# Two transformer blocks on one core: the gates' chains interleaved, signals per block, entry rows on ScalarE, the store in parts

## The reference, cut to what matters

```
for layer in range(2):
    hl = modulate(rmsnorm(xl, norm_g[layer, 0]), mod_l[0], mod_l[1])   # and hc from xc
    yc, yl = even_mixer(...) if layer % 2 == 0 else rwkv_mixer(...)
    xl = xl + mod_l[2] * rmsnorm(yl, norm_g[layer, 1])
    hl = modulate(rmsnorm(xl, norm_g[layer, 2]), mod_l[3], mod_l[4])
    xl = xl + mod_l[5] * rmsnorm(conv_ffn(hl, ...), norm_g[layer, 3])
    ...   # the same for xc and hc, where not last
rwkv_project: xx = shifted - h;  xr, xw, xk, xv, xa, xg = (h + xx * mu[i] for i in range(6))
```

## Time and profile before

| | |
|---|---|
| median of 3 runs | 3086.62 us (3085.43 to 3086.74) |
| profiled execution: its own time, its span | 3089.13 us, 3087.3 us |
| busy: TensorE, VectorE, ScalarE | 2873.1 us (93%), 1645.6 us (53%), 1219.4 us (39%) |
| mean granted clock of TensorE | 0.957 of full |
| bytes moved by DMA | 349.82 MB, 113 GB/s on average |

### The profile page before, as it was taken

One profiled execution on the slowest core, in us unless ns is written; L12 is line 12 of the kernel. 1 busy time (PEld: TensorE's weight loads), 2 busy tenths in 40 slices (PEclk: granted clock), 3 DMA queues, 4 the chain that ended last, 5 costly groups with the idle time before them and its releaser, 6 DMA issues.

```text
span 3087.3 us, 64784 instructions
## 1 busy us (share of the span) xinstructions
PE 2873.1 (93%) x27888; PEld 2405.2 (78%) x27888; DVE 1645.6 (53%) x2475; ACT 1219.4 (39%) x1856; POOL 112.9 (4%) x152
## 2 busy tenths in 40 slices
PE   8999999999999997998877999997998999998997
PEld 8977799899777996776656777784456998985986
DVE  5546555455465544312564777646233554565885
ACT  5445554444455444323443432333203434432333
POOL 0000000000000000000000000000001222220000
PEclk9999999999999998997988999998999999999999
DMA  6544345455443543541001243321210000002442
GB/s 247 184 170 167 123 164 182 166 184 184 170 161 117 178 175 115 188 151 69 2 10 55 106 154 138 121 86 48 96 44 26 5 4 24 5 4 110 148 146 103
DMA packets 49981, 349.82 MB, mean 113 GB/s; under 512 B 5793, under 2 KB 5793, under 8 KB 9249
## 3 DMA queue, kind: packets, MB, share of 16 engines
q1 hardware_dynamic: 49248, 343.56, 31.3%
q0 software_dynamic: 448, 2.11, 0.2%
HBM read 344.61 MB, written 1.05 MB: 112 GB/s over the span
## 4 chain that ended last, share of the span: by engine, by line
PE 80%; DVE 13%; ACT 4%; issue 2%; DMA 1%; DVEq 0%; ACTq 0%; SPq 0%
PE psum L165 79%; DVE arena L98 3%; DVE ring_low L87 2%; DVE arena L87 2%; DVE wide L87 1%; ACT w_high L144 1%; ACT arena L140 1%; DMA ring<-in_evt 1%; PE psum L170 1%; DVE wide L98 1%; ACT x_high L138 1%; DVE ring L87 0%; ACT L138 0%; DVE h L98 0%; ACT arena L144 0%
## 5 line engine op out<-in xcount | busy, mean ns | idle before, releaser
L87 DVE TENSOR_TENSOR ring_low<-ring,w_high 128x2048 fp32r<-128x2048 f32 (+3 forms) x254 | 560.3, 2206 | 565.3 <-ACT w_high L144 560.8
L144 ACT ACTIVATE w_high<-ring 128x2048 fp32r<-128x2048 f32 (+3 forms) x254 | 468.9, 1846 | 794.9 <-PE psum L165 482.6
L165 PE MATMUL psum<-x_high,w_high 128*128 128x256 f32 (+1 forms) x2040 | 634.5, 311 | 11.9 <-DVE x_low L87 6.5
L165 PE MATMUL psum<-x_high,ring_low 128*128 128x256 f32 (+1 forms) x2040 | 627.5, 308 | 0.0
L165 PE MATMUL psum<-x_low,w_high 128*128 128x256 f32 (+1 forms) x2040 | 627.3, 308 | 0.0
L165 PEld LDWEIGHTS psum<-x_high,w_high 128*128 128x128 f32 x2040 | 390.9, 192 | 50.1 <-issue 17.1
L165 PEld LDWEIGHTS psum<-x_high,ring_low 128*128 128x128 f32 x2040 | 390.8, 192 | 18.6
L165 PEld LDWEIGHTS psum<-x_low,w_high 128*128 128x128 f32 x2040 | 390.9, 192 | 16.9
L165 PE MATMUL psum<-wide,ring 64*64 64x64 f32 (+3 forms) x3888 | 385.2, 272 | 19.2 <-DVE wide L98 9.7
L165 PEld LDWEIGHTS psum<-wide,ring 64*64 64x64 f32 (+2 forms) x3888 | 270.7, 147 | 115.4 <-issue 90.8
L165 PE MATMUL psum<-w_high,x_high 128*128 128x512 f32 (+2 forms) x720 | 281.3, 391 | 9.9 <-issue 8.0
(11 more groups left out here) (196 smaller groups left out, 3444.1 us busy)
## 6 DMA issues: line engine op xcount, KB each, us to landing
ring<-in_f_gu SPq DMA_DIRECT2D x88, 1024.0 KB, 4.8
ring<-in_w_mod SPq DMA_DIRECT2D x48, 1024.0 KB, 5.0
ring<-in_fu SPq DMA_DIRECT2D x44, 1024.0 KB, 4.9
ring<-in_f_dn SPq DMA_DIRECT2D x40, 1024.0 KB, 4.8
ring<-in_w_in SPq DMA_DIRECT2D x28, 1024.0 KB, 4.8
ring<-in_fd SPq DMA_DIRECT2D x20, 1024.0 KB, 4.9
ring<-in_rkvr SPq DMA_DIRECT2D x12, 1024.0 KB, 4.8
ring<-in_w_out SPq DMA_DIRECT2D x8, 1024.0 KB, 4.8
```

What stands on the lines that cost most here:

```text
L87: self.done(self.eng.tensor_tensor(o, a, b, op), then)
L144: self.done(self.eng.activation(o, i, ACT.Copy, scale=scale), then)
L165: ins = self.eng.matmul(o, l, r, start=a, stop=z)
```

## The change

Five things:

- Gates that come in pairs (before FFN 4 and before the recurrent mixer): the context gate's squares, factors and products of half n=1 are done between the copies of the latent gate's blocks. `gates_end` then orders VectorE: additions of the context gate, factors of the latent one between them, one product, the first norm's factors, the other product, the additions of the latent gate, the second norm's factors. ScalarE's root of the latent gate lies between the squares of the first norm.
- The signals of squares (`gs_ok`) and additions (`ga_ok`) are given per token block. The small Sqrt stands before the squares of half n=0, for all gates but the latent one of evo.
- The single gates (recurrent mixer, FFN 5): token block 0 of half 1 is multiplied ahead of the factors. The clearing of the image tiles for FFN 5 moves from its start to the end of the recurrent mixer.
- RAW norms: all eight rows k are written by ScalarE; `norm_rows` goes. VectorE's differences wait for pairs of rows or single rows, and the mixes are made between them. The norm before FFN 5 joins `SHARED`. The RAW norms' scratch moves to another buffer.
- The store of `h` goes out in four DMAs of 256 KB, each behind its addition.

```diff
 CONV = (("c", 4, 1), ("c", 4, 0))
-SHARED = (("e", 1), ("e", 0)) + CONV
+SHARED = (("e", 1), ("e", 0)) + CONV + (("c", 5, 0),)
...
 xt_mm = signal("xt_mm", [(q, k) for q in NORMS for k in range(8)])
-xh_ok = signal("xh_ok", [(q, k) for q in NORMS for k in range(0, 8, 2 if q in RAW else 1)])
+xh_ok = signal("xh_ok", [(q, k) for q in NORMS for k in range(8)])
 xw_ok = signal("xw_ok", [(q, k) for q in SHARED for k in (0, 2, 4, 6)])
-xr_ok = signal("xr_ok", [(q, k) for q in RAW for k in (1, 3, 5, 7)])
...
+    if q == ("c", 5, 0):
+        return x_whole[:, k, :]
...
         se.wait_ge(*md_ok[1 if q[0] == "r" or q[1] == 5 else 0, 1 if q[0] == "c" else 0])
-    for k in range(0, 8, 2 if q in RAW else 1):
+    for k in range(8):
...
     if i == 4:
-        A.act(nsmall(CONV[0])[:, 20:21], ident[:, 0:1], ACT.Sqrt)
-        for q in CONV:
-            norm_squares(A, q, 0)
-            norm_squares(A, q, 1)
-            norm_root(A, q)
+        norm_squares(A, CONV[0], 0)
+        gate_root(A, GATES[1])
+        norm_squares(A, CONV[0], 1)
+        norm_root(A, CONV[0])
+        for n in range(2):
+            norm_squares(A, CONV[1], n)
+        norm_root(A, CONV[1])
...
                 A.copy(CY[:, tb, 512 * n:512 * n + 512], bank(down_bank(i, n, tb)), ya_ok((i, n, tb)))
-    for q in GATED[i]:
-        gate_squares(A, q, 1)
-    for q in GATED[i]:
-        gate_root(A, q)
+                if n and tb == 0:
+                    gate_squares(A, GATED[i][0], 1)
+    if i >= 4:
+        gate_root(A, GATED[i][0])
+    if i == 4:
+        gate_squares(A, GATED[i][1], 1)
...
     norms = norms_of(i)
-    if i == 5:
-        D.fill(IMG, 0.0)
-        D.fill(IMC, 0.0, cleared(i))
...
             D.copy(CY[:, tb, 512 * n:512 * n + 512], bank(down_bank(i, n, tb)), yd_ok((i, n, tb)))
-    if i != 4:
-        gates_dve(D, GATED[i])
+            if i == 4 and n and tb == 1:
+                gate_factors(D, GATES[2])
+                gate_mult(D, GATES[2], 1)
+            if i == 5 and n:
+                gate_mult(D, GATES[5], 1, (0,))
+                gate_end(D, GATES[5])
...
     dst, y, col, w, scr, sm, b = gate_of(q)
-    if n:
+    if n == 0 and (q[0], q[-1]) != ("e", 0):
...
         A.eng.wait_ge(*gate_ready(q, n, j))
-        A.act(scr, y[:, j, 512 * n:512 * n + 512], ACT.Square, gs_ok((q, n)) if j else None, scale=1.0 / 32,
+        A.act(scr, y[:, j, 512 * n:512 * n + 512], ACT.Square, gs_ok((q, n, j)), scale=1.0 / 32,
...
-def gate_mult(D, q, n):
+def gate_mult(D, q, n, js=TWO):
     dst, y, col, w, scr, sm, b = gate_of(q)
-    D.eng.wait_ge(*gs_ok[q, n])
     D.eng.wait_ge(*gb_mm[q, n])
-    for j in TWO:
+    for j in js:
+        D.eng.wait_ge(*gs_ok[q, n, j])
...
     sm = gate_of(q)[5]
-    D.eng.wait_ge(*gs_ok[q, 1])
+    D.eng.wait_ge(*gs_ok[q, 1, 1])
...
     D.recip(sm[:, 8:10], sm[:, 4:6], gm_ok(q))
-    gate_mult(D, q, 1)
...
         D.stt(d, y[:, j, 512 * n:512 * n + 512], sm[:, 8 + j:9 + j], d, ALU.mult, ALU.add,
-              ga_ok((q, n)) if j else None)
-
-def gates_dve(D, qs):
-
-    for q in qs:
-        gate_factors(D, q)
-    for q in qs:
-        for n in TWO:
-            gate_add(D, q, n)
+              ga_ok((q, n, j)))
+
+def gate_end(D, q):
+
+    gate_factors(D, q)
+    gate_mult(D, q, 1, (1,))
+    for n in TWO:
+        gate_add(D, q, n)
+
+def gates_end(D, one, other, norms):
+
+    gate_add(D, one, 0)
+    gate_factors(D, other)
+    gate_add(D, one, 1)
+    gate_mult(D, other, 1, (0,))
+    norm_factors(D, norms[0])
+    gate_mult(D, other, 1, (1,))
+    for n in TWO:
+        gate_add(D, other, n)
+    norm_factors(D, norms[1])
...
             A.copy(YO[:, tb, 512 * n:512 * n + 512], bank(4 * n + tb), eo_a((n, tb)))
-    for q in GATES[0:2]:
-        gate_squares(A, q, 1)
-    for q in GATES[0:2]:
-        gate_root(A, q)
+            if n and tb == 0:
+                gate_squares(A, GATES[0], 1)
+    gate_root(A, GATES[0])
+    gate_squares(A, GATES[1], 1)
...
             D.copy(YO[:, tb, 512 * n:512 * n + 512], bank(4 * n + tb), eo_d((n, tb)))
-    for q in GATES[0:2]:
-        gate_factors(D, q)
-    gate_add(D, GATES[0], 0)
-    gate_add(D, GATES[0], 1)
-    gate_add(D, GATES[1], 0)
-    norm_factors(D, CONV[0])
-    gate_add(D, GATES[1], 1)
-    norm_factors(D, CONV[1])
+            if n and tb == 1:
+                gate_factors(D, GATES[0])
+                gate_mult(D, GATES[0], 1)
+    gates_end(D, GATES[0], GATES[1], CONV)
...
     se = A.eng
-    A.act(nsmall(RAW[0])[:, 20:21], ident[:, 0:1], ACT.Sqrt)
-    for n in TWO:
-        norm_squares(A, RAW[0], n)
+    norm_squares(A, RAW[0], 0)
+    gate_root(A, GATES[3])
+    norm_squares(A, RAW[0], 1)
...
     ve = D.eng
-    for q in GATES[2:4]:
-        gate_factors(D, q)
-    gate_add(D, GATES[2], 0)
-    gate_add(D, GATES[2], 1)
-    gate_add(D, GATES[3], 0)
-    norm_factors(D, RAW[0])
-    gate_add(D, GATES[3], 1)
-    norm_factors(D, RAW[1])
+    gates_end(D, GATES[2], GATES[3], RAW)
     D.tsc(okv, kv[:, 1, :], -1.0, 1.0, ALU.mult, ALU.add)
-    norm_rows(D, RAW[0])
-    ve.wait_ge(*xh_ok[RAW[0], 6])
...
         a, b = max(n, 0), 256 + min(n, 0)
+        ve.wait_ge(*xh_ok[RAW[0], 2 * q + 1])
...
         D.tsc(XX[:, 2 * q:2 * q + 2, e:e + 1], XT[:, 2 * q:2 * q + 2, e:e + 1], -1.0, None, ALU.mult, None)
-    norm_rows(D, RAW[1])
-    ve.wait_ge(*xh_ok[RAW[1], 6])
     for c in FOUR:
+        ve.wait_ge(*xh_ok[RAW[1], c])
...
         D.tsc(d[:, :, e:e + 1], s[:, :, e:e + 1], -1.0, None, ALU.mult, None)
+        D.stt(XM[0][:, c, :], XX[:, c, :], mu[:, 4, c:c + 1], XT[:, c, :], ALU.mult, ALU.add, mix_ok((4, c)))
     for q, n in ((2, 64), (3, -64)):
+        ve.wait_ge(*xh_ok[RAW[1], 2 * q + 1])
...
         D.tsc(XX[:, 2 * q:2 * q + 2, e:e + 64], XT[:, 2 * q:2 * q + 2, e:e + 64], -1.0, None, ALU.mult, None)
-    for k in range(8):
-        D.stt(XM[0][:, k, :], XX[:, k, :], mu[:, 4, k:k + 1], XT[:, k, :], ALU.mult, ALU.add, mix_ok((4, k)))
+        for k in (2 * q, 2 * q + 1):
+            D.stt(XM[0][:, k, :], XX[:, k, :], mu[:, 4, k:k + 1], XT[:, k, :], ALU.mult, ALU.add, mix_ok((4, k)))
...
     lead(outputs_dve(D, 0), outputs_dve(D, 1))
+    D.fill(IMG, 0.0)
+    D.fill(IMC, 0.0, cleared(5))
...
     for n in TWO:
+        if n:
+            gate_mult(D, GATES[4], 1, (0,))
...
         if n == 0:
-            gate_mult(D, ("r", 0), 0)
-    gates_dve(D, GATES[4:5])
+            gate_mult(D, GATES[4], 0)
+    gate_end(D, GATES[4])
...
         eng.dma_start(raw(key), src).then_inc(slot_in[slot_of[key]], 16)
-    eng.wait_ge(*ga_ok[("c", 5, 0), 1])
-    eng.dma_start(out, h[:, :, :]).then_inc(stored, 16)
-    eng.wait_ge(stored, 16)
+    for n in TWO:
+        for j in TWO:
+            half = slice(512 * n, 512 * n + 512)
+            eng.wait_ge(*ga_ok[("c", 5, 0), n, j])
+            eng.dma_start(out[:, j, half], h[:, j, half]).then_inc(stored, 16)
+    eng.wait_ge(stored, 64)
...
```

More of the change, by code:

```diff
@@ L457, in scratch_of @@
             if q in RAW:
-                x = XMAT[0]
+                x = XMAT[1]
                 d = x[:, 256 * q[1]:256 * q[1] + 256]
@@ L494, in rows_ready @@
             s = SOURCE[q]
-            return h_ok[s, n, t] if s in STAGES else ga_ok[s, n]
+            return h_ok[s, n, t] if s in STAGES else ga_ok[s, n, t]
         def norm_bank(q, k):
@@ L554, in norm_factors @@
                 D.tsc(scratch_of(q)[0][:, t, :], ident, sm[:, 16 + t:17 + t], None, ALU.mult, None, xs_ok((q, t)))
[L556 to L561, removed]
         def norm_dve(D, q):
@@ L581, in norm_dve @@
                 else:
-                    x = x_whole[:, k, :] if q == ("c", 5, 0) else ntmp[:, :]
+                    x = whole_of(q, k) if q == ("c", 5, 0) else ntmp[:, :]
                     D.tsc(x, p, scale(k), shift(k), ALU.mult, ALU.add)
@@ L598, in norm_pe @@
                 b = norm_bank(q, k)
-                T.bank(b, (xr_ok if k % 2 else xh_ok)[q, k] if q in RAW else xl_ok[q, k])
+                T.bank(b, xh_ok[q, k] if q in RAW else xl_ok[q, k])
                 for t in range(2):
@@ L1503, in mod_final @@
             D.tt(mD[:, 2 * i + 1, :, :], mT[l][:, 3 * i + 2, :, :], bc(ng2[:, l, 2 * i + 1, :], 2), ALU.mult, md_ok((l, i)))
-        gb_mm, ga_ok = [signal(x, [(q, n) for q in GATES for n in TWO]) for x in ("gb_mm", "ga_ok")]
+        gb_mm = signal("gb_mm", [(q, n) for q in GATES for n in TWO])
+        ga_ok = signal("ga_ok", [(q, n, j) for q in GATES for n in TWO for j in TWO])
         BESIDE = (GATES[0:2], GATES[2:4], GATES[4:5], GATES[5:6])
-        gs_ok, gd_ok = [signal(x, [(q, n) for qs in BESIDE for n in TWO for q in qs]) for x in ("gs_ok", "gd_ok")]
+        gs_ok = signal("gs_ok", [(q, n, j) for qs in BESIDE for n in TWO for q in qs for j in TWO])
+        gd_ok = signal("gd_ok", [(q, n) for qs in BESIDE for n in TWO for q in qs])
         gm_ok, gr_ok = [signal(n, GATES) for n in ("gm_ok", "gr_ok")]
```

## The result

The changed kernel takes 3070.27 us (median of 5 runs, 3068.53 to 3072.32) beside 3086.62 for the kernel before on the same chip: a ratio of 0.9948, 95% interval 0.9934 to 0.9963, or 11 to 20 us less. It is faster, 2.3 us above the forecast of 3068.0 and inside its range of 3063.5 to 3073.5. The profiled execution took 3071.02 with a span of 3069.2, against 3087.3.

The account below looks back on a forecast made before the run. TensorE bounds the kernel, so work elsewhere pays only where it stands still, at four joins. 2.8 + 11.0 - 0.4 + 2.4 + 1.6 + 1.2 = 18.6 us less than 3086.62 gives 3068.0; 8-in-10 range 3063.5 to 3073.5.

Parts of the forecast that it names:

- Rival 4: The joins shorten, but later work waits for weights, so the total stays within 0.2% of before; chance 0.04.
- Join A: Evo output to FFN 4: gate work between the copies brings the second norm's factors earlier, -2.8 us.
- join C: Recurrent output to FFN 5: a product ahead of the last copy and shared norm rows, together -2.4 us.
- Join B, gates: FFN 4 to the recurrent mixer, up to the latent norm's factors: reordered gates and moved table load, -3.7 us.
- Join B, entry: Recurrent mixer's entry: ScalarE makes all 16 rows, TensorE's low-rank product follows the mixes; -7.3 us, with the gates -11.0.
- The clock alternative: TensorE at half clock when the low-rank product starts: 1.75 us a step until 2139.0, caught up by 2143.4.
- Rival 1: Recurrent mixer's entry pays less, mixes in effect waiting for the last latent row: B -6.7, total 3072.3 us; chance 0.08.
- The moved load: FFN 4's table load, moved ahead of group 9's high copy, stalls TensorE: 1.73 us against 1.34 slack, +0.4.
- Rival 2: The moved load stalls more, every step behind it slipping too: 2 to 3 us, total 3070.5; chance 0.06.
- Join D: Last products to the end of the store: table load and one product leave the path, additions end -1.6 us.
- The store: Kernel's end: four 256 KB parts, each landing in 2.7 us instead of 3.9 whole; -1.2 us, bounds 0 and -2.1.
- Rival 5: TensorE stays at half clock in the projections behind the entry: slower, 3124 us if the k-projection is wholly so; chance 0.02.

Follow-up runs that it names:

- the seventh experiment: The changed kernel, but VectorE's differences of the latent rows all wait for ScalarE's last latent row; 3072.68 us, one execution, before 3084.96.
- the eighth: The changed kernel, but the eight mixes come after all differences, rows staying with ScalarE; 3074.09 us, one execution, before 3084.96.
- load early: The changed kernel with FFN 4's table load moved ahead of the weight split of group 10; 3066.78 us in one execution, 3069.41 as median of 6.
- first row early: The load early kernel with the context norm's first row written ahead of the latent squares at A and B; median 3068.12 us, ratio 0.9941.
- experiments 1 to 4: In order: entry as before, store whole, load late, load early, each an edit of the changed kernel; 3072.61, 3074.12, 3071.72 and 3066.78 us.
- entry as before: The changed kernel with only the RAW norms' rows, differences and mixes put back as before; 3072.61 us, one execution, before 3082.41.
- load late: The changed kernel with the table load of FFN 4's gates back at the second half; 3071.72 us, one execution, before 3082.41.
- store whole: The changed kernel with the output stored in one DMA of 1024 KB behind the last addition; 3074.12 us, one execution, before 3082.41.

## Why the prediction was right, point by point

- **What bounds it.** Right. The stops of TensorE at four joins were the place, and the gains add up there. Rival 4 (nothing comes through) is out: from A's last copy, SyncE's next 30 issues in the changed kernel stand 2.74 earlier than before, all alike, and the ratio is clear of 1 in both timings.
- **Join A** -2.71 for -2.8, and **join C** -2.4 for -2.4. The order of operations came out as written; hand-overs were 0.1.
- **Join B, gates** -3.47 for -3.7. The hand-overs were rounded down: the first addition starts 1.65 behind TensorE's end and not 1.54, and from there to the factors it is 10.75 and not 10.6.
- **Join B, entry** -6.65 for -7.3, the largest miss. The last context pair ended where it was put (6.8 behind the factors). From the first latent difference (2130.20) to the eighth mix's end (2139.62 plus two mixes, 2141.2) it is 11.0, not 10.7, since the single-row pattern repeats every 1.52, not 1.45; and TensorE ends 1.2 behind it, not 0.9. The clock alternative (TensorE at half from the first mix) did not occur: 1.00 in the window above. My sum had it catch up by the end, and the seventh experiment, where it did occur, bears that out; in the eighth, where the mixes come close together, it costs an estimated 2.1. Rival 1 (the mixes wait for the last latent row) is out: the first latent difference starts 6.9 behind the factors, when ScalarE's rows still run for 4.3 (to 2134.46).
- **The moved load** +0.84 for +0.4. The lateness against the release was right: the low part ends at 2083.26, 0.41 behind the release of group 8 (2082.85). But the release is the wrong mark, as it comes when TensorE's last product ends. The products overlap: they start 0.23 apart while each lasts 0.39, so the next one would have started at 2082.66, 0.19 ahead of the release. To that come 0.14 of hand-over (it starts at 2083.40) and 0.08 because the second product follows the first by 0.31 and not 0.23. 0.19 + 0.41 + 0.14 + 0.08 is 0.82 of the 0.84: this term of the sum was mis-sized by where the slack was measured to. By the Trainium skill ("ScalarE: Activation LUTs", What ACT_TABLE_LOAD costs) a drain of about 1380 ns would have come on top of the load; the row at 2075.20, 0.01 behind the load's end, shows none, as the rows of before did not, and ahead of the load there is none either (the split ends at 2073.89, the load starts at 2073.91). Rival 2 asked for 2 to 3 us and for later groups slipping as well; the next release follows 10.88 behind group 9's, so they don't.
- **Join D** -1.51 for -1.6. **The store** -1.77 for -1.2: inside its bounds of 0 and -2.1, nearer the lower price. A 256 KB store lands in 2.1, where the 256 KB load that I priced it by took 2.7. The rule to batch to at least 1 MiB (the Trainium skill, "DMA: Bandwidth & Descriptors", Bandwidth) speaks of throughput and does not decide here: the last quarter alone sets the end.
- **Rival 5** (half clock in the projections) is out: the granted clock is 1.00 in every window from 2150 to 2240, and its mean over the kernel is 0.963, before 0.957.
- **The total.** For the profiled execution the forecast was 3070.5, and it took 3071.02: 0.9 more by the sizes above, 0.4 less by the stretches that the forecast took as fixed. The median lies further off, 2.3, because the forecast carried over the 2.5 by which the profiled execution before stood above its median, and the one after stands 0.75 above its own. That the total came so close is in part luck: two timings of the changed kernel gave 3070.27 and 3068.64. What bears the prediction out is the intervals.

## What to carry to other kernels

Price a chain at a join operation by operation in the order of each queue, add 0.1 for every hand-over, and check it by the interval between two rows: such an interval repeats to some hundredths where the total moves by microseconds. A late signal is paid once for every queue that stands behind it. Measure the slack of an operand of TensorE to the start of the product that needs it, not to the release of the weights before it: those two lay 0.19 apart. Let the consumer follow the producer piece by piece, and start it early: behind a gap of 1.83 us TensorE kept its full clock, behind 6.11 and 6.31 us it came back at half. That costs where the pieces then come faster than it works at half clock, and nothing where they come slowly enough for it to catch up.

## What the hardware showed beside that

**The clock's return after a stop moves between kernels.** Inside FFN 4, from 287 to 290 us behind A's last copy on, TensorE stops for 6.62 us in every kernel and comes back at half clock. How many products it then makes slowly is not the same. Windows of 6 us from the first product behind the stop; the column behind the engines is the granted clock. Before, changed, load early, first row early:

```profile
1982.30:1988.30 6.00, 6.00 (x18) 4.78 (x19) 4.58 (x2) 2.08 (x2) 0.00 (x0) 0.66 0.00 0
```

```profile
1979.13:1985.13 6.00, 6.00 (x16) 4.75 (x17) 4.58 (x2) 2.16 (x2) 0.00 (x0) 0.59 0.00 0
```

```profile
1979.30:1985.30 6.00, 6.00 (x20) 4.87 (x21) 4.59 (x2) 2.01 (x2) 0.00 (x0) 0.73 0.00 0
```

```profile
1978.43:1984.43 6.00, 6.00 (x15) 4.77 (x16) 4.58 (x2) 2.14 (x2) 0.00 (x0) 0.53 0.00 0
```

It makes 9, 11, 7 and 13 products at half clock, each 0.2 longer, so the same stop costs the changed kernel 0.4 more than before, the load-early one 0.4 less. Two executions of the changed kernel both had 11, and two of the load-early one both 7. It is not the work ahead of the stop that sets the number: seven of the kernels do the same up to there (the changed one and experiments 1 to 4, 7 and 8), the stop begins 287.2 us behind A's last copy in all of them, and they have 11 (changed, entry as before, load late), 7 (load early, and experiments 7 and 8) and 6 (store whole, whose edit lies at the very end). So a difference of some tenths, up to about 1 us, can stand far from an edit, ahead of it too. Whether it belongs to the kernel or to the moment is not settled by two kernels that repeated their number.

**Where the kernels part, and where executions of one kernel do.** From the end of the low-rank product on, before, changed, load-early and first-row-early kernels run alike to 0.02 us for 199 us. Then TensorE enters the recurrence at half clock, and the moment at which it rises differs. Windows in the recurrence, before and changed, both from 213.6 us behind that end:

```profile
2368.00:2374.00 6.00, 5.69 (x184) 5.58 (x182) 3.06 (x6) 1.96 (x4) 1.67 (x3) 0.95 0.01 3
```

```profile
2356.00:2362.00 6.00, 6.00 (x156) 6.00 (x154) 2.65 (x5) 1.13 (x3) 1.67 (x3) 0.70 0.01 3
```

Around there the changed kernel falls 1.3 us behind. But this is not where executions of one kernel part. The changed kernel's two executions and one of the load-early kernel have the same 0.70 in that window, and GpSimd's instructions start at the same distance from the low-rank product's end to 0.03 us until 250 us behind it; at 258 us the first difference appears (0.4 between the two of the changed kernel), and all three have been at full clock (1.00 in every window of 6 us) since 219. From there on the engines' order shifts against each other and they drift apart: from the entry's end to the first output weights it is 416.10 and 416.85 for the changed one, twice, 414.30 before, and 412.8 to 417.0 over all the changed kernel's variants. What starts this drift within one kernel no run here shows.
